# Attention values stacked in one stationary tile, the low part moved to the accumulator's other half

## What is computed

```python
z = q @ k.T * 64 ** -0.5                      # per head, s < t only
log_beta = log_sigmoid(z)
log_fail = where(causal, log_beta - z, 0)
survive = reverse_cumsum(log_fail) - log_fail
a = where(causal, exp(log_beta + survive), 0)
o = a @ v                                      # (528, 64) per head
y_conv = b_c * causal_conv3(c_c * h_c)
```

## Time and profile before

| what | value |
|---|---|
| three timed runs | 1968.05, 1967.29, 1967.72 us |
| the profiled execution | 1968.2 us, of which the span is 1966.5 us |
| TensorE matmul busy | 1800.2 us, 92% of the span |
| VectorE, ScalarE, GpSimd busy | 56%, 46%, 12% |
| granted TensorE clock, mean | 0.965 |

### The profile page before, as it was taken

The page is one execution under the profiler, slowest core; times in us unless marked ns, Lnnn a source line. Parts: engine busy times, 40 slices in busy tenths (PEclk is TensorE's granted clock), DMA queues, the critical chain, the costliest instruction groups (busy, mean ns, idle before and its releaser), DMA issues.

```text
span 1966.5 us, 30973 instructions
## 1 busy us (share of the span) xinstructions
PE 1800.2 (92%) x11869; PEld 1587.3 (81%) x11869; DVE 1109.3 (56%) x1596; ACT 902.1 (46%) x1190; POOL 229.9 (12%) x347
## 2 busy tenths in 40 slices
PE   5999999999999987999999967587979999999996
PEld 4899999999999986999988835466757777778884
DVE  4455555655333347555542278999577767654443
ACT  4566676666333344333332242234455555643332
POOL 0011111101000010000000008687000000000001
PEclk8999999999999998999999988789989999999998
DMA  3222222222223351232233237121212122133332
GB/s 115 83 77 74 73 66 85 73 76 77 76 85 91 112 183 44 87 95 93 89 97 97 84 117 129 34 52 36 75 33 75 60 76 68 48 113 107 124 101 96
DMA packets 64721, 166.02 MB, mean 84 GB/s; under 512 B 21956, under 2 KB 22148, under 8 KB 64520
## 3 DMA queue, kind: packets, MB, share of 16 engines
q1 hardware_dynamic: 64648, 165.03, 27.6%
HBM read 154.23 MB, written 8.41 MB: 83 GB/s over the span
## 4 chain that ended last, share of the span: by engine, by line
PE 59%; DVE 22%; ACT 8%; issue 7%; DMA 3%; POOL 1%; SPq 0%; ACTq 0%; DVEq 0%
PE J L750 25%; PE J L989 13%; PE J L762 6%; PE J L960 6%; DMA WR<-weights 2%; DVE WL L1695 2%; DVE VR L1976 1%; DVE VI L1976 1%; PE J L1156 1%; POOL E L2365 1%; ACT E L1306 1%; ACT E L1302 1%; DVE TS L1976 1%; PE Z L836 1%; DVE Q2L L1699 1%
## 5 line engine op out<-in xcount | busy, mean ns | idle before, releaser
L1695 DVE TENSOR_TENSOR WL<-WR,WH 128x1024 fp32r<-128x1024 f32 x271 | 336.6, 1243 | 315.2 <-ACT WH L1235 306.5
L1235 ACT ACTIVATE WH<-WR 128x1024 fp32r<-128x1024 f32 x271 | 285.4, 1054 | 218.2 <-DMA WR<-weights 75.2
L750 PE MATMUL J<-XH,WH 128*128 128x264 f32 (+1 forms) x1376 | 286.2, 290 | 25.3 <-DVE XL L1699 17.6
L750 PE MATMUL J<-XH,WL 128*128 128x264 f32 (+1 forms) x1376 | 281.1, 286 | 0.0
L750 PE MATMUL J<-XL,WH 128*128 128x264 f32 (+1 forms) x1376 | 281.0, 286 | 0.0
L750 PEld LDWEIGHTS J<-XH,WH 128*128 128x128 f32 x1376 | 217.0, 191 | 31.3 <-issue 20.1
L750 PEld LDWEIGHTS J<-XL,WH 128*128 128x128 f32 x1376 | 216.0, 191 | 0.0
L750 PEld LDWEIGHTS J<-XH,WL 128*128 128x128 f32 x1376 | 215.5, 191 | 0.0
L2384 POOL TENSOR_TENSOR SA<-SQ 128x512 f32<-128x512 f32 (+1 forms) x3 | 3.9, 1294 | 1020.3 <-ACT SQ L1471 511.9
L2365 POOL TENSOR_SCALAR_AFFINE_SELECT E<-E 128x128 f32<-128x128 f32 (+1 forms) x160 | 51.5, 358 | 446.3 <-DVE E L1767 238.5
L989 PE MATMUL J<-X2H,WH 128*128 128x512 f32 x168 | 71.0, 423 | 8.9 <-DVE X2L L2021 8.8
(11 more groups left out here) (438 smaller groups left out, 4298.2 us busy)
## 6 DMA issues: line engine op xcount, KB each, us to landing
WR<-weights SPq DMA_DIRECT2D x271, 512.0 KB, 3.5
X<-tokens SPq DMA_DIRECT2D x4, 528.0 KB, 5.9
H<-tokens SPq DMA_DIRECT2D x8, 264.0 KB, 4.0
res_dram<-H SPq DMA_DIRECT2D x1, 2048.0 KB, 8.9
u_dram<-UT SPq DMA_DIRECT2D x8, 256.0 KB, 2.2
US<-u_dram SPq DMA_DIRECT2D x16, 128.0 KB, 6.1
gate_dram<-GST SPq DMA_DIRECT2D x8, 256.0 KB, 2.2
GSB<-gate_dram SPq DMA_DIRECT2D x8, 256.0 KB, 3.7
```

Source lines behind the costliest of these rows:

```text
L750: mm = pe.matmul(o[:, 512 * h:512 * h + half], ws[:, s, w], xs[:, a:a + half], start=(k == 0 and i == 0), stop=(k == 7 and i == 2))
L1235: act.activation(WH[:, n % SPLIT, :], WR[:, n % RAW, :], ACT.Copy).then_inc(w_hi, 1)
L1695: dve.tensor_tensor(WL[:, n % SPLIT, :], WR[:, n % RAW, :], WH[:, n % SPLIT, :].bitcast(F32), ALU.subtract).then_inc(w_lo, 1)
```

## The change

- The low and high halves of a head's values become one stationary tile: `VW[p, kt, head, x, 64]`, x = 0 high, x = 1 low. One matmul gives high-half rows 0 to 63 and low-half rows 64 to 127; `values` takes two passes, `AH` and `AL`, instead of three. The product low by low comes with it.
- The two halves have to be added. `head_part` (ScalarE) copies rows 64 to 127 to a new SBUF tile `OT`, between Exp and Ln of the next softplus. `head_sum` (VectorE) adds rows 0 to 63 from PSUM, ahead of its softplus, and releases the accumulator. `head_out` (ScalarE) copies `OT` to `OH` after `fail_hi`; `head_lo` (VectorE) subtracts to `OL` after `fail_lo`.
- ScalarE's copy of the c job to `CT` moves ahead of `fail_hi`; VectorE's `YL` moves ahead of softplus(h + 1); in m = 0 the release by a nop moves ahead of softplus too.
- Condition rows are staged in `MROW1`, since `OT` lies where `MROW` is.
- In `gates(0)` TensorE waits for `o_lo` (the low part of the last head) ahead of the attention output's job.

```diff
--- before.py
+++ after.py
...
@@ -243,8 +248,7 @@
         AL = sb("AL", [P, SCORE], A0 + 12 * SCORE, F32R)
         A1 = A0 + 16 * SCORE
         QS = [sb("QS0", [P, L1], A1, F32R), sb("QS1", [P, L1], A1 + 2112, F32R)]
-        VH = sb("VH", [P, 5 * P], A1 + 4224, F32R)
-        VL = sb("VL", [P, 5 * P], A1 + 6784, F32R)
+        VW = sb("VW", [P, 5, 2, 2, 64], A1 + 4224, F32R)
         assert A1 + 9344 <= U[8]
 
         M0 = U[8]
...
@@ -865,8 +875,8 @@
                 for kt, a, b, c in parts:
                     half = a // HALF
                     at = 512 * half - HALF * half
-                    for vs, ps in ((VH, AH), (VH, AL), (VL, AH)):
-                        mm = pe.matmul(o[:, at + a:at + b], vs[:, kt * P:(kt + 1) * P], ps[:, c + a:c + b],
+                    for ps in (AH, AL):
+                        mm = pe.matmul(o[:, at + a:at + b], VW[:, kt, h % 2].rearrange("p x d -> p (x d)"), ps[:, c + a:c + b],
                                        start=half not in seen, stop=True, skip_group_check=True)
                         seen.add(half)
                 mm.then_inc(pv_done, 1)
@@ -922,7 +932,7 @@
                     pe.wait_ge(y_lo, DT)
                     job(n + 2, t_gate(m, 2), YH, YL, start=LIVE, half=HALFK)
                     values(HEADS - 1, T_GATE + 2)
-                    pe.wait_ge(read_out[slot(T_GATE + 2)], nth(T_GATE + 2) + 1)
+                    pe.wait_ge(o_lo, HEADS)
                 else:
                     job(n, t_gate(m, 0), XH, XL, start=LIVE, half=HALFK)
                     job(n + 1, t_gate(m, 1), XH, XL, start=LIVE, half=HALFK)
@@ -1293,7 +1303,7 @@
             split_hi(SPLIT)
             k_hi_(T_MIX + 2, N_MIX + 1)
 
-            def softplus(h):
+            def softplus(h, between=None):
 
                 h = as_lin(h)
                 act.wait_ge(z_done, val(h + 1))
@@ -1302,6 +1312,8 @@
                 act.activation(E[:], Z[:, 0:SCORE], ACT.Abs).then_inc(soft_step, 1)
                 act.wait_ge(soft_step, val(3 * h + 1))
                 act.activation(E[:], E[:], ACT.Exp, scale=-1.0).then_inc(soft_step, 1)
+                if between is not None:
+                    between()
                 act.wait_ge(soft_step, val(3 * h + 2))
                 act.activation(E[:], E[:], ACT.Ln, bias=1.0).then_inc(soft_step, 1)
 
@@ -1331,8 +1343,16 @@
 
                 h = as_lin(h)
                 r = slice(64 * (h % 2), 64 * (h % 2) + 64)
+                act.wait_ge(o_sum, val(h + 1))
+                act.activation(OH[r, cols(m * L1, L1)], OT[r], ACT.Copy).then_inc(o_hi, 1)
+
+            def head_part(h, t):
+                h = as_lin(h)
+                r = slice(64 * (h % 2), 64 * (h % 2) + 64)
                 act.wait_ge(pv_done, val(h + 1))
-                act.activation(halves(OH[r, cols(m * L1, L1)]), JV[as_lin(t) % 2][r], ACT.Copy).then_inc(o_hi, 1)
+                if positive(h):
+                    act.wait_ge(o_lo, val(h))
+                act.activation(halves(OT[r]), JV[as_lin(t) % 2][64:P], ACT.Copy).then_inc(o_part, 1)
 
             def mix(m, last=False):
                 n, t, h = N_MIX + 2 + 8 * m, T_MIX + 10 * m, 2 * m
@@ -1347,20 +1367,20 @@
                     act.wait_ge(vt_done, val(m))
                 act.activation(halves(VT[:]), src, ACT.Copy).then_inc(read_out[(t + 4) % 2], 1)
                 split_hi(n + 4)
-                softplus(h)
-                if later:
-                    head_out(h - 1, m - 1, t + 5)
-                fail_hi(h)
+                softplus(h, (lambda: head_part(h - 1, t + 5)) if later else None)
                 src = job_result(t + 6, n + 1)
                 if positive(m):
                     act.wait_ge(y_lo, val(m))
                 act.activation(halves(CT[:]), src, ACT.Copy).then_inc(read_out[(t + 6) % 2], 1)
+                fail_hi(h)
+                if later:
+                    head_out(h - 1, m - 1, t + 5)
                 split_hi(n + 5)
                 act.wait_ge(vt_done, val(m + 1))
                 if positive(h):
                     act.wait_ge(pv_done, val(h))
-                act.activation(VH[:, 0:4 * P], J[(t + 7) % 2][:, 0:4 * P], ACT.Copy)
-                act.activation(VH[0:META, 4 * P:], J[(t + 7) % 2][0:META, 4 * P:5 * P], ACT.Copy).then_inc(v_hi, 1)
+                act.activation(VW[:, 0:4, :, 0], heads(J[(t + 7) % 2][:, 0:4 * P]), ACT.Copy)
+                act.activation(VW[0:META, 4:5, :, 0], heads(J[(t + 7) % 2][0:META, 4 * P:5 * P]), ACT.Copy).then_inc(v_hi, 1)
                 split_hi(n + 6)
                 split_hi(n + 7)
                 split_hi(n + 8)
@@ -1370,9 +1390,9 @@
 
                 act.wait_ge(read_out[slot(t + 9)], nth(t + 9) + 1)
                 act.activation(YH[:, cols(m * L1, L1)], CT[:], ACT.Copy).then_inc(y_hi, 1)
-                softplus(h + 1)
+                softplus(h + 1, lambda: head_part(h, t + 10))
+                fail_hi(h + 1)
                 head_out(h, m, t + 10)
-                fail_hi(h + 1)
                 if not last:
                     q_hi(m + 1, t + 11, n + 6)
                     split_hi(n + 10)
@@ -1402,6 +1422,7 @@
                     weight_exp(HEADS - 1)
                     weight_hi(HEADS - 1)
                     split_hi(n + 6)
+                    head_part(HEADS - 1, T_GATE + 2)
                     head_out(HEADS - 1, DT - 1, T_GATE + 2)
                 else:
                     split_hi(n + 5)
...
@@ -1796,12 +1816,19 @@
                 dve.wait_ge(a_hi, val(h + 1))
                 low(AL[:], E[:], AH[:]).then_inc(a_lo, 1)
 
-            def head_out(h, m, t):
+            def head_sum(h, t):
                 h, t = as_lin(h), as_lin(t)
                 r = slice(64 * (h % 2), 64 * (h % 2) + 64)
+                dve.wait_ge(o_part, val(h + 1))
+                dve.tensor_tensor(halves(OT[r]), JV[t % 2][0:64], halves(OT[r]), ALU.add).then_inc(o_sum, 1)
+                dve.wait_ge(o_sum, val(h + 1))
+                dve.nop().then_inc(read_out[t % 2], 1)
+
+            def head_lo(h, m):
+                h = as_lin(h)
+                r = slice(64 * (h % 2), 64 * (h % 2) + 64)
                 dve.wait_ge(o_hi, val(h + 1))
-                low(halves(OL[r, cols(m * L1, L1)]), JV[t % 2][r], halves(OH[r, cols(m * L1, L1)]))\
-                    .then_inc(read_out[t % 2], 1)
+                low(OL[r, cols(m * L1, L1)], OT[r], OH[r, cols(m * L1, L1)]).then_inc(o_lo, 1)
 
             def mix(m, last=False):
                 n, t, h = N_MIX + 2 + 8 * m, T_MIX + 10 * m, 2 * m
@@ -1811,23 +1838,25 @@
                 if later:
                     weight_lo(h - 1)
                 split_lo(n + 4)
-                softplus(h)
                 if later:
-                    head_out(h - 1, m - 1, t + 5)
+                    head_sum(h - 1, t + 5)
                 else:
                     dve.nop().then_inc(read_out[(t + 5) % 2], 1)
+                softplus(h)
                 fail_lo(h)
+                if later:
+                    head_lo(h - 1, m - 1)
                 split_lo(n + 5)
                 dve.wait_ge(v_hi, val(m + 1))
-                low(VL[:, 0:4 * P], J[(t + 7) % 2][:, 0:4 * P], VH[:, 0:4 * P])
-                low(VL[0:META, 4 * P:], J[(t + 7) % 2][0:META, 4 * P:5 * P], VH[0:META, 4 * P:])\
+                low(VW[:, 0:4, :, 1], heads(J[(t + 7) % 2][:, 0:4 * P]), VW[:, 0:4, :, 0])
+                low(VW[0:META, 4:5, :, 1], heads(J[(t + 7) % 2][0:META, 4 * P:5 * P]), VW[0:META, 4:5, :, 0])\
                     .then_inc(read_out[(t + 7) % 2], 1)
                 split_lo(n + 6)
                 split_lo(n + 7)
                 dve.wait_ge(job_done, val(n + 4))
                 if positive(m):
                     dve.wait_ge(mod_saved, val(16 * m))
-                dve.tensor_copy(MROW[0:2, 0:2 * P], ZT[0:2, 0:2 * P]).then_inc(mod_rows, 1)
+                dve.tensor_copy(MROW1[0:2], ZT[0:2, 0:2 * P]).then_inc(mod_rows, 1)
 
                 dve.wait_ge(job_done, val(n + 5))
                 dve.wait_ge(read_out[slot(t + 6)], nth(t + 6) + 1)
@@ -1843,11 +1872,12 @@
                 dve.tensor_tensor(halves(CT[:]), JV[(t + 9) % 2], halves(CV[:]), ALU.mult)\
                    .then_inc(read_out[(t + 9) % 2], 1)
                 split_lo(n + 9)
-                softplus(h + 1)
                 dve.wait_ge(y_hi, val(m + 1))
                 low(YL[:, cols(m * L1, L1)], CT[:], YH[:, cols(m * L1, L1)]).then_inc(y_lo, 1)
-                head_out(h, m, t + 10)
+                head_sum(h, t + 10)
+                softplus(h + 1)
                 fail_lo(h + 1)
+                head_lo(h, m)
                 if not last:
                     q_lo(m + 1, t + 11)
                     split_lo(n + 10)
@@ -1887,7 +1917,9 @@
                    .then_inc(read_out[tc % 2], 1)
                 split_lo(n + 6)
                 if first:
-                    head_out(HEADS - 1, DT - 1, T_GATE + 2)
+                    head_sum(HEADS - 1, T_GATE + 2)
```

(21 more changed lines are left out.)

## The result

| | before | after |
|---|---|---|
| median of four runs | 1967.88 us | 1993.73 us |
| ratio, 95% interval | | 1.0123 [1.0104, 1.0142] |
| profiled execution, span | 1968.2, 1966.5 us | 1993.66, 1991.2 us |

The forecast was 1975.0 us with a range to 1980. The sign was right, and the size was three and a half times too small.

What follows compares the result with a forecast made beforehand. TensorE and the loop over ScalarE, VectorE, GpSimd and weight DMA were both taken to be at the limit. 1968.2 + 4.3 without the clock + 3.0 for the clock = 1975.5, median 0.5 lower: 1975.0 us, range 1966.5 to 1980.

Steps and rivals of the forecast that it cites:

- TensorE's part: Values product: nine matmuls fewer, 3.18 to 2.14 us; were TensorE alone the bound, an iteration would lose 2.4 us.
- Both ways at the limit, a gain of one brings next to nothing: Loop: TensorE and the other engines' loop both at the limit, slack 0.14 us; shortening one alone brings nothing.
- The even chain: Even head: copy before Ln and subtraction behind `GL` delay `AL` 0.61 + 0.61 = 1.22 us; new stall of 2.1 us.
- The strided writes: `VW` writes keep runs of 64 elements: put at zero, at most 0.2 us more on each low part.
- The masks: Odd head: masks fall from 1.58 to 1.18 us, -0.40, as `YL` now lies before the maximum.
- The odd chain and the v job: Odd head: steps sum to 2.05 us at the first `KL`; v job at 275.66, iteration 0.67 us longer.
- m = 0: First iteration: odd head shifts 0.83 us, v job starts at 107.25 in place of 107.77: -0.5 us.
- The second stall: Before the v job, released by `KL`: TensorE idle 1.0 us, or none where the clock fell.
- The end: Head 15's values to the job on the attention output: 4.76 us becomes 5.10, +0.3 us.
- The sum without the clock: Whole kernel: -0.5 + 6 x 0.67 + 0.5 + 0.3 = +4.3 us.
- The clock: Loop: half the stalls of about 2 us followed by 3.4 us at 1.2 GHz, +0.75 each, four of eight iterations: +3.0 us.
- Rival 2: Clock falls at every stall and strided writes cost: 8 x 0.75 + 4.3 = 10.3 us and more, 1979 to 1981; chance 0.10.

Runs made afterwards that it cites:

- The stacking alone: Changed kernel with head_out copying and subtracting rows 0 to 63 in its old places, upper rows not added: 1974.22 us, 1.0021 of before.
- the moved line alone: Kernel before the change, with ScalarE's high part of weight block n + 8 moved behind the even head's weight exponential: 1967.36 us, 0.9982 of before.
- all steps in cover: Changed kernel with block n + 8's high part, upper rows' copy, sum, `YH`, `YL` and both heads' low parts moved later: 1958.13 us, 0.9945 of before.
- `fill`: Changed kernel with 18 matmuls nobody reads ahead of each even head's values product: 1986.33 us, 1.0083 of before.
- both stalls filled: Changed kernel with 18 unread matmuls ahead of even heads' values and 11 ahead of each v job from m = 1: 1980.85 us, 1.0053 of before.
- `split_later`: Changed kernel with ScalarE's high part of weight block n + 8 moved behind the even head's weight exponential: 1965.82 us, 0.9979 of before.

## Why the prediction was wrong

The step that failed is the price of the clock. Point by point, by the prediction's own steps:

- *TensorE's part*: 2.14 us per product; measured 2.13 (head 5, at the full clock: 234.72 to 236.85). Right.
- *Both ways at the limit, a gain of one brings next to nothing*: right, and shown from both sides. The stacking alone did not gain, the moved line alone brought 0.2%, and together, with all steps in cover, they gave 0.55%.
- *The even chain*, +1.22 us, stall of 2.1: measured +1.36 and 2.2. `head_lo` put 0.85 us between `GL` and split(n + 5) in place of 0.61. The two kinds of head differ here, which the prediction's row (264.04 to 264.65) could not show. In the even head's stage `head_lo` works on the odd head's rows 64 to 127, and seven times in seven it starts 0.63 us after `GL` and split(n + 5) 0.74 after it; on rows 0 to 63 it starts 0.52 after `GL` eight times in eight, and there the added time is the 0.61. The strided writes were put at zero, and `VW`'s low part takes 0.87 us against 0.88.
- *The masks*, -0.40: right, 1.58 became 1.18 in every odd head.
- *The odd chain and the v job*: by the prediction's own rows +0.67 should read +0.76. The second `KL` ends at 275.60, and with the hand-over of 0.14 the v job starts at 275.74, not 275.66 (the same slip stands in m = 0). The second stall was forecast at 1.0 us "or none there, where the clock fell". It is absent in the changed kernel, and 1.37 us where the first is filled. Without falls an iteration costs 1.0 to 1.2 us more than before (56.7 and 56.9 against 55.7).
- *m = 0*: forecast -0.5. Where no fall is added in it (`fill`) that is right: from m = 0's v job to the next it is 57.28 us against 57.76. In the changed kernel it is 60.73, with the stall ahead of head 1's scores and 10.2 us at half the clock.
- *The end*: from the values of head 15 to the job on the attention output it was to be 5.10 us, and is 5.12 (525.30 to 530.42).
- *The sum without the clock*, +4.3, should have been about +8. From the first v job of the loop to the attention output's job the run with both stalls filled takes 467.9 us against 457.9 before. Of these 10 us, 1.7 are a fall of 3.4 us left in m = 0. With the clock's term as forecast that would have given some 1979 us, within the range.
- *The clock*, +3.0 us: this is the step that failed. It said: "of stalls of about 2 us I let half be followed by such a fall", 3.4 us long, and netted 0.75 us for each. All eight were followed by one, of 6.8 or 10.2 us. Over the stretch just named the changed kernel takes 481.3 us, 13.4 more than with both stalls filled; the two kernels' times differ by 13. So the term is +13 in place of +3. Per iteration it is 58.6 (the mean of the seven from head 0 to head 14: (498.97 - 88.67) / 7) less 56.9, so 1.7 to 1.8 us. The size can be worked out from the rows: of 6.8 us at 1.2 GHz some 6.3 lie behind the stall of head 6 and cost 3.15, and 1.37 of that takes the place of the second stall. The price that the prediction took came from three idle stretches in other places of the kernel, and nothing there said that it held in this loop.
- *Rival 2* had a fall at every stall, and ended at 1981. With 6.8 us in place of 3.4 behind each, 8 x 1.7 more on its 1978, it would have come to 1992; that is an estimate after the fact.

Adding up: +8.3 without the clock, +13.4 for the falls at the stalls, +1.7 for the fall left in m = 0 are the loop's 23.4 us; the rest of the span, outside the loop, is 1.3 us longer, and why was not looked into.

Which stalls the clock falls behind stays open. The length of the stall does not decide by itself. Before the even heads' values, idle stretches of 0.2 to 0.9 us with the scores straight ahead of them had a fall seven times in seven in the stacking alone; two of 0.2 us in the same place had none in `split_later`; eight of 0.4 to 1.05 us with nine idle-time matmuls straight ahead had one. The stall of 1.44 us at the end had a fall in the kernel before and none in the same kernel with the line moved. The prediction gave rival 2 as its reason that the bursts on either side of the stall are short. These runs neither show that nor rule it out.

## What to carry to other kernels

In a loop where TensorE is 99% busy, look first how close the other engines' chain comes to it: here 0.14 us, so that 17 us of saved matmuls were worth nothing until the steps of that chain had been moved into idle time. A stall that is added to a loop at the full clock has two prices, the longer chain and the fall of the clock behind the stall. The second can be the larger (here 1.7 to 1.8 us per iteration against 1.0 to 1.2), and it repeats in each iteration, so a forecast should carry the case that every stall pays it, at more than the length seen elsewhere. Matmuls that nobody reads are a cheap test of the second price (13 us here), and where a stall cannot be removed, a repair.

## What was not expected of the hardware

- Eight stalls of 2.2 us in a loop otherwise busy cost 61 us at half the clock (65 us against 3.4 us before, loop and gate together).
- In the stacking alone, idle stretches of 0.2 to 0.9 us before the values product each had a fall behind them (7 of 7), while two of 0.2 us in the same place of another run had none. Ahead of the v job, 1.2 to 1.4 us were followed by a fall in 7 of 7, 1 of 6 and 2 of 6 iterations in three kernels. Which it is could not be settled.
- Two short subtractions of the same size on VectorE cost 0.61 us on rows 0 to 63 and 0.85 us on rows 64 to 127 between their neighbours. The trace shows it in fifteen heads out of fifteen; their neighbours differ as well, so that the cause is not shown.
